# Sending twelve of 144 expert weight transfers as three pieces of rows each, in a one-core diffusion-transformer kernel

## What is computed

```python
def swiglu(h, w1, w3, w2):
    return (jax.nn.silu(h @ w1) * (h @ w3)) @ w2
# layer 1, D = 1024, D_FF = 2816, 8 experts, top 2
logits = (h @ moe_router[i]).astype(jnp.float32)
top_val, top_idx = lax.top_k(logits, TOP_K)
gate = jax.nn.softmax(top_val, axis=-1)
...
for e in range(N_EXPERTS):
    out = out + weight[..., e:e + 1] * swiglu(h, moe_w1[i, e], moe_w3[i, e], moe_w2[i, e])
```

## Time and profile before

| What | Value |
|---|---|
| median of 3 runs | 1776.65 us (1773.91 to 1778.34) |
| the profiled execution | 1776.37 us |
| its span in the trace | 1774.6 us |
| PE (matmul) busy | 1683.9 us, 95% |
| DVE busy, ACT busy | 698.5 us, 420.9 us |
| SP's and most other data (queue q1) | 399.47 MB, 56.2% of 16 engines' time |
| instruction fetches (queue q8) | 134 packets, 2.20 MB |

### The profile page before, as it was taken

One profiled execution on the slowest core, in us unless ns is written; L12 is line 12 of the kernel. 1 busy time (PEld: TensorE's weight loads), 2 busy tenths in 40 slices (PEclk: granted clock), 3 DMA queues, 4 the chain that ended last, 5 costly groups with the idle time before them and its releaser, 6 DMA issues.

```text
span 1774.6 us, 38447 instructions
## 1 busy us (share of the span) xinstructions
PE 1683.9 (95%) x17608; PEld 1311.2 (74%) x17608; DVE 698.5 (39%) x978; ACT 420.9 (24%) x579; POOL 48.0 (3%) x60
## 2 busy tenths in 40 slices
PE   7999999999899999999999898999999998999976
PEld 3777766788688888886977787776666796699744
DVE  5447656444533333897764664211111011001013
ACT  4233244323422222223533543000000000000001
POOL 0000000002000000220000000000000000000000
PEclk9999999999999999999999998999999999999999
DMA  9731212135323333685323249799999999999995
GB/s 391 300 110 55 100 48 65 52 110 193 121 95 118 120 122 117 253 293 217 119 96 100 95 157 415 286 406 426 428 428 427 427 428 428 428 427 428 428 427 230
DMA packets 46754, 439.79 MB, mean 248 GB/s; under 512 B 5361, under 2 KB 5617, under 8 KB 12418
## 3 DMA queue, kind: packets, MB, share of 16 engines
q1 hardware_dynamic: 40034, 399.47, 56.2%
q0 software_dynamic: 5552, 34.90, 5.4%
q10 hardware_dynamic: 1008, 3.02, 0.4%
HBM read 433.83 MB, written 3.54 MB: 246 GB/s over the span
## 4 chain that ended last, share of the span: by engine, by line
PE 81%; DMA 7%; DVE 6%; ACT 3%; issue 3%; DVEq 0%; SPq 0%; ACTq 0%
PE psum L2280 19%; PE psum L1782 14%; PE psum L1784 14%; PE psum L1783 14%; PE psum L2299 9%; DMA expert_units<-in_moe_up 4%; DMA expert_units<-in_moe_w 2%; DMA expert_units<-in_moe_up_rest 2%; ACT units_hi L710 1%; DVE units_lo L1100 1%; PE psum L2021 1%; PE psum L2043 1%; PE psum L1827 1%; PE psum L2257 1%; PE psum L2001 1%
## 5 line engine op out<-in xcount | busy, mean ns | idle before, releaser
L2280 PE MATMUL psum<-expert_units,gathered 128*32 128x256 f32 (+1 forms) x8064 | 411.0, 362 | 17.7 <-DMA expert_units<-in_moe_up_rest 8.1
L2280 PEld LDWEIGHTS psum<-expert_units,gathered 128*32 128x32 f32 x8064 | 310.5, 110 | 113.8 <-issue 16.2
L1782 PE MATMUL psum<-h_hi,units_hi 128*128 128x512 f32 (+1 forms) x928 | 345.2, 372 | 10.6 <-DVE h_lo L1182 5.3
L1784 PE MATMUL psum<-h_hi,units_lo 128*128 128x512 f32 (+1 forms) x928 | 337.0, 363 | 0.0
L1783 PE MATMUL psum<-h_lo,units_hi 128*128 128x512 f32 (+1 forms) x928 | 336.8, 363 | 0.0
L1100 DVE TENSOR_TENSOR units_lo<-raw_units,units_hi 128x2048 fp32r<-128x2048 f32 (+2 forms) x88 | 175.2, 1991 | 259.5 <-ACT units_hi L710 259.5
L710 ACT ACTIVATE units_hi<-raw_units 128x2048 fp32r<-128x2048 f32 (+2 forms) x88 | 147.2, 1673 | 410.4 <-PE psum L1784 354.1
L1782 PEld LDWEIGHTS psum<-h_hi,units_hi 128*128 128x128 f32 x928 | 177.2, 191 | 50.9 <-issue 22.4
L2299 PE MATMUL psum<-expert_units,expert_midT 128*32 128x256 f32 x3600 | 204.0, 382 | 11.0 <-DMA expert_units<-in_moe_w 6.6
L1784 PEld LDWEIGHTS psum<-h_hi,units_lo 128*128 128x128 f32 x928 | 176.9, 191 | 27.3
L1783 PEld LDWEIGHTS psum<-h_lo,units_hi 128*128 128x128 f32 x928 | 177.3, 191 | 24.6
(11 more groups left out here) (329 smaller groups left out, 1681.5 us busy)
## 6 DMA issues: line engine op xcount, KB each, us to landing
expert_units<-in_moe_up SPq DMA_DIRECT2D x64, 2048.0 KB, 25.2
expert_units<-in_moe_w SPq DMA_DIRECT2D x40, 2048.0 KB, 26.8
expert_units<-in_moe_up_rest SPq DMA_DIRECT2D x32, 1536.0 KB, 27.0
raw_units<-in_w_in SPq DMA_DIRECT2D x40, 1024.0 KB, 4.9
raw_units<-in_ffn_w SPq DMA_DIRECT2D x22, 1024.0 KB, 4.9
mod_units<-in_w_mod_rows POOLq DMA_DIRECT2D x20, 1024.0 KB, 5.9
raw_units<-in_ffn_w SPq DMA_DIRECT2D x16, 704.0 KB, 4.9
raw_units<-in_w_pab SPq DMA_DIRECT2D x16, 512.0 KB, 3.5
```

Of the source, the lines that this page charges most:

```text
L1782: MM(o, wh, xh, start=first, stop=False)
L1784: return MM(o, wl, xh, start=False, stop=last)
L2280: ins = MM(o[GRP * q:GRP * (q + 1), :], G[:, k, at, GRP * rr:GRP * (rr + 1)], W[:, kk, q, :], start=k == 0 and rr % 2 == 0, stop=k == DK - ...
```

## The change

Twelve full units are sent as three transfers each: rows 0 to 111, rows 112 to 119 and rows 120 to 127. They are the first unit of down round 0 of each of the eight experts, and the second unit of up3's round 1 of experts 1, 3, 5 and 7, which stands directly before it in the order. So the units from 8 on to 133 and 134 are concerned. Each piece raises the slot's semaphore by 16, so TensorE now waits for 16 times the number of pieces that the slot has had. What is loaded, into which slot, and the order of the units stay as they were.

```diff
+THIRDS = {FIRST[e_, "down", 0] for e_ in range(NE)} | {FIRST[e_, "up3", 1] + 1 for e_ in range(1, NE, 2)}
+ROW_CUTS = ((0, 112), (112, 120), (120, 128))
+
+
+def row_parts(n):
+
+    return ROW_CUTS if n % N_EXPERT_UNITS in THIRDS else ((0, P),)
+
+
+def parts_landed(n):
+
+    return sum(len(row_parts(m)) for m in range(n % RING, n + 1, RING))
...
                         into, src = ering[n % RING][:, 0:ks * 4 * width], expert_unit(w, who, at_unit)
-                        sp.dma_start(into, src).then_inc(e_in[n % RING], 16)
+                        for first, end in row_parts(n):
+                            sp.dma_start(into[first:end], src[first:end]).then_inc(e_in[n % RING], 16)
...
                 def arrived(n):
-                    pe.wait_ge(e_in[n % RING], 16 * (n // RING + 1))
+                    pe.wait_ge(e_in[n % RING], 16 * parts_landed(n))
```

## The result

The changed kernel takes 1908.69 us (median of 4 runs, 1903.23 to 1918.32) against 1776.55 us for the kernel before, 1.0746 times as long (95% interval 1.0722 to 1.077). I had forecast 1770.3 us with a range of 1768 to 1786, so both the sign and the size were wrong. The profiled execution has a span of 1916.5 us, 141.9 more than before.

The account below looks back on a forecast made before the run. The prediction took eight late DMA engines at the end of the expert stream as the bound; moving rows shifts 7.35 us, of which 6.2 us is gained: 1776.37 - 6.2 = 1770.2 us (stated as 1770.3), range 1768 to 1786.

Parts of the forecast that it names:

- What bounds the kernel: End of the expert stream: eight of sixteen DMA engines 13.8 us behind set the last landings; instruction fetches inferred as cause.
- The price of a row and the shift: Twelve units at 0.612 us per row: 7.35 us less on eight engines, 7.35 us more on the other eight.
- I take 112 rows as 7 for each of sixteen engines: In the cut units, the 112-row transfer gives each engine 7 rows, against 8 in a full unit.
- 0.612 to 2.45 us for a row: Row time in the eight-row pieces: from the usual 0.612 us to 2.45 us, if four rows are served in turn.
- the lower bound: Rows of the eight-row pieces cost 0.612 us as ever; taken because 96-row stores left the stream at 428 GB/s.
- The first rival: At the stream's end, engines receiving extra rows are some of the late ones: 7.35 us later, 1783.7 us; chance 0.14.
- 6.2 us to win: At the end of the stream, the predicted gain, of the 7.35 us moved, if the receivers are the early eight.
- The hint that I used: At the start, the engine taking the single-row bias load took none of four instruction fetches; receivers likelier than even not late.
- The second rival: In the eight-row pieces, rows to neighbouring partitions delay each other: 1814 us, mild form 1785; chance 0.22.
- The third: Load doesn't move: pieces cut over all sixteen engines, or imbalance re-forms behind SP's issues; 1776.4 us, chance 0.12.
- the vanished shelf: Sign at the stream's end: DMA share 0.50 for some 10 us, to go if right, stay if no load moves.
- What was at nothing: Costs taken as zero: SP's 24 more issues (8 us without cover) and small closing packets (1.5 us at a tenth row each).

Follow-up runs that it names:

- the 112-row transfer alone: Against the changed kernel, the twelve units load only rows 0 to 111, with no small pieces; 1888.3 us, kernel before 1778.2.
- the drained halves: Twelve units as rows 0 to 63 and 64 to 127, queue run empty around each; 1894.0 us, against 1841.7 with whole units and the same waits.
- the even and odd rows: Against the kernel before, twelve units as 64 even and 64 odd partitions; 1773.8 us against 1778.0, in twelve more runs 1777.9 against 1777.8.
- The halves: Against the kernel before, twelve units as rows 0 to 63 and rows 64 to 127; 1899.7 us, +121.
- the pair of near and spread pieces: Against the kernel before: twelve units' last 512 columns in sixteen 8-row transfers, on neighbouring partitions (1804.5 us) or every fourth partition of 32 (1808.8 us).
- the low and high runs: Twelve units as 128 rows of half the columns plus eight 8-row transfers, on partitions 0 to 63 (1778.9 us) or 64 to 127 (1826.2 us).
- the run with the eights low: Against the kernel before: twelve units as 128 rows of half the columns plus eight 8-row transfers on partitions 0 to 63, rest left out; 1778.9 us.
- the column cut: Against the kernel before, twelve units cut by columns: 128 rows of the first 3584, 128 rows of the last 512; 1776.5 us, before 1775.5.
- run 96: Not a run number: 96 counts added transfers. Twelve units, half the columns whole, eight 8-row transfers on partitions 0 to 63; 1778.9 us, before 1778.0.

## Why the prediction was wrong, point by point

**What bounds the kernel** held. The late engines set the end: in the run with 29 us of relief for most of them, the few that got none still set it. (The sum came to 1770.2 us, the last line says 1770.3; nothing hangs on it.)

**The price of a row and the shift** held only as arithmetic. The shift of 12 x 0.612 us assumes that a row's time is a constant of the engine. It is 0.612 us in full units, and about twice that once cut units are in flight.

**"I take 112 rows as 7 for each of sixteen engines"** is the step that failed. The count may well be right; what I left out is where each engine's seven rows go. I put the question of place to the eight-row pieces alone, and let the 112-row transfer pass as the old one less a row. The runs show in its place that 110 of the 132 us come with the 112-row transfer alone, and only some 20 with the pieces. The bounds "0.612 to 2.45 us for a row" stood on 16 rows of a unit and belonged on all 128. At 1.21 us a row, as in the drained halves, a unit's own rows cost 12 x 8 x 0.6 = 58 us. The rows around a cut unit, which I had at nothing, bring the rest. Why the rows of the 112-row transfer are slow, though they go to nearly all partitions, stays open: that engines meet there is my inference, and the same inference doesn't say why the even and odd rows are free, since there too the engines would leave their own partitions.

**The reason for taking the lower bound** was weak: the 96-row stores leave the rate at 428 GB/s, but they read SBUF, and they are 2% of the traffic in their window. A row that covers the opposite direction at a fiftieth of the load bounds nothing.

The Trainium skill's page "SBUF — State Buffer", section "Door 1: The DMA port swizzle", says that partitions 0 to 63 reach only eight of sixteen DMA ports. The halves agree (184 GB/s from 1307 to 1312 us, under half of 428), and so do the even partitions, which reach all ports (426 GB/s). The 112 rows reach all of them too and ran at 197 to 216 GB/s, so the rule alone doesn't cover the main loss. I had weighed this rule for the pieces only. For them it would give an estimated quarter of the rate (two ports for eight engines), and the pair of near and spread pieces, 1804.5 and 1808.8 us, doesn't show that. The page "DMA: Bandwidth & Descriptors", section "The descriptor swizzle", gives the pattern by which a 128-row transfer has each engine write to a port of its own; the low and high runs agree with it, 1778.9 against 1826.2 us.

**The first rival** (receivers are some of the late engines, 0.14) came true beside the collisions. I had written that it decides as soon as one engine is in both sets; the run with the eights low shows two. Late and early aren't the two sets of the change: six givers and two receivers are late, if eight are late in all. So even free of collisions the change had no 6.2 us to win, and by my own price would have lost 7.35. The hint that I used, one engine missed by four fetches, said nothing of the other seven.

**The second rival** (0.22) was the nearest: right in its sign (a loss in the middle of the stage, right behind the moved units), likely right in kind (engines in one another's way at the target), wrong in place for five sixths of the loss, and too small: 1814 us against 1909. For the pieces it gave up to 44 us, and they brought some 20. **The third** (nothing moves) isn't refuted by the vanished shelf, which went in the halves too. It is out by the run with the eights low: had each 8-row transfer been cut over all sixteen engines, all would have been relieved alike and eight would still have been late.

**What was at nothing.** SP's issues and the small packets cost next to nothing: the column cut has 12 more transfers (1776.5 against 1775.5 us), the low run 96 more (1778.9 against 1778.0). TensorE's clock I had only as a part of the spread; it cost 42 us, because it fell to 1.2 GHz after pauses in the middle of the stage.

What stays open: no view numbers engines, so which of them fetch instructions was never seen. The packet records of before do bear out the sum, though. The 80 fetches between 1200 and 1760 us last 0.88 to 0.97 us, in an order of lengths that repeats every eight fetches, and the row that starts as a fetch ends is some 0.5 us too long. That is 1.4 us per fetch, or 14 us for ten fetches on each of eight engines, beside the 13.8 us by which eight are late. That the fetches take turns on just these eight is an estimate from it. That seven neighbouring rows go to each engine in the 112-row transfer is inferred; no run shows it. Whether a shift to the early engines alone, with no slow rows, would gain 6 us wasn't tried; 8-row transfers can't do it, because two of their engines are late ones. Most kernels ran once; the differences read from single runs are 20 us and more, against up to 8 us among the runs of before (1774.19 to 1782.36).

## What to carry to other kernels

A transfer that isn't all 128 rows isn't "the same with fewer rows": price all of its rows anew, and not only those that were cut off. If a large transfer must be cut, cut it by columns or into even and odd partitions; both cost nothing here, and cutting off the last 16 rows of twelve of 144 transfers cost 6 to 7.5%. When a share of 0.50 says that eight engines are late, find out which before loading the rest: a test that only relieves the suspected ones is cheap and shows at the end of the stream who is left.

## What the runs showed of the hardware that was not expected

A row of 16 KB lasted 0.612 us in full units, and 1.36 to 1.43 us on average when cut units were in flight, at a DMA share of 1.0: the share doesn't show it, only the GB/s do. One cut unit held the rate at 170 to 293 GB/s for 25 us; with the queue drained around the cut units a cut cost 4.4 us. 64 rows in one half of the partitions ran at under half rate, 64 even rows at full rate (184 and 426 GB/s).
